# A decoder step on one core: page blocks side by side in the compression stage, low halves and bias copies on other engines, a third raw buffer

## What is computed

```
h = rmsnorm(x, norm_mix_g)                       # 1056 rows, transposed
cmp_rows = h @ w_in[:, cmp columns] + b_in       # 256 columns
# compression of every 32 rows (CMP_BLOCK) of keys and values, for the
# prompt's rows and for the 8 x 1024 past rows in paged caches
blk  = rows.reshape(B, nc, 32, 2, 2, 64) + pe[:, :, None, :]
flat = transpose(blk, (0, 1, 3, 4, 2, 5)).reshape(B, nc, 2, 2, 32 * 64)
hid  = gelu(einsum('bnzgf,zfe->bnzge', flat, w1))
out  = einsum('bnzge,zef->bnzgf', hid, w2)
```

## Time and profile before

| | |
|---|---|
| median of 3 runs | 2277.45 us (2276.51 to 2278.89) |
| the profiled execution, its own time | 2273.18 us |
| its span, first to last instruction | 2271.0 us |
| mean granted clock of TensorE | 0.957 |
| PE busy | 2137.8 us (94%) |
| DVE, ACT, POOL busy | 869.9, 686.7, 342.7 us |
| DMA | 153.41 MB, mean 68 GB/s |

### The profile page before, as it was taken

One profiled execution on the slowest core, in us unless ns is written; L12 is line 12 of the kernel. 1 busy time (PEld: TensorE's weight loads), 2 busy tenths in 40 slices (PEclk: granted clock), 3 DMA queues, 4 the chain that ended last, 5 costly groups with the idle time before them and its releaser, 6 DMA issues. The chain is left out here.

```text
span 2271.0 us, 36952 instructions
## 1 busy us (share of the span) xinstructions
PE 2137.8 (94%) x14615; PEld 1494.9 (66%) x14615; DVE 869.9 (38%) x1713; ACT 686.7 (30%) x1270; POOL 342.7 (15%) x253
## 2 busy tenths in 40 slices
PE   6999989799999998999999799886999999999998
PEld 5796645577777777556666566554666666666666
DVE  6321041465656564545334454233222222222223
ACT  4221232255555554362332233112111101101211
POOL 4300032400000000001011111004402501501400
PEclk8968999899999999999999899988999999999999
DMA  7601362211111102203102343311111111111101
GB/s 221 171 29 48 114 179 87 88 39 39 39 39 39 39 30 57 62 19 105 43 12 72 91 148 109 114 37 37 56 47 46 50 52 46 46 55 46 46 28 76
DMA packets 198941, 153.41 MB, mean 68 GB/s; under 512 B 10320, under 2 KB 185574, under 8 KB 198634
## 3 DMA queue, kind: packets, MB, share of 16 engines
q1 hardware_dynamic: 189386, 138.96, 20.6%
q0 software_dynamic: 4640, 10.60, 1.7%
q10 hardware_dynamic: 4800, 2.30, 0.3%
HBM read 124.66 MB, written 31.33 MB: 69 GB/s over the span
## 5 line engine op out<-in xcount | busy, mean ns | idle before, releaser
L318 PE MATMUL ps<-hH,wH 128*128 128x352 f16 x1584 | 324.8, 314 | 24.3 <-DVEq L283 19.9
L318 PE MATMUL ps<-hH,wL 128*128 128x352 f16 x1584 | 324.4, 314 | 0.0
L318 PE MATMUL ps<-hL,wH 128*128 128x352 f16 x1584 | 324.2, 314 | 0.0
L297 DVE SCALAR_TENSOR_TENSOR wL<-w,wH 128x1024 f16<-128x1024 f32 x98 | 120.0, 1225 | 288.6 <-ACT wH L290 273.1
L318 PEld LDWEIGHTS ps<-hH,wH 128*128 128x128 f16 x1584 | 154.9, 98 | 110.3 <-issue 25.3
L318 PEld LDWEIGHTS ps<-hL,wH 128*128 128x128 f16 x1584 | 155.3, 98 | 82.7
L318 PEld LDWEIGHTS ps<-hH,wL 128*128 128x128 f16 x1584 | 155.2, 98 | 82.4
L318 PE MATMUL ps<-mH,wH 128*128 128x352 f16 x960 | 196.4, 314 | 7.9 <-DVEq L283 6.9
L318 PE MATMUL ps<-mL,wH 128*128 128x352 f16 x960 | 196.1, 313 | 0.0
L318 PE MATMUL ps<-mH,wL 128*128 128x352 f16 x960 | 196.0, 313 | 0.0
L290 ACT ACTIVATE wH<-w 128x1024 f16<-128x1024 f32 x98 | 102.5, 1046 | 231.1 <-PE ps L318 225.4
(11 more groups left out here) (424 smaller groups left out, 3081.7 us busy)
## 6 DMA issues: line engine op xcount, KB each, us to landing
w<-in_mlp_w SPq DMA_DIRECT2D x64, 512.0 KB, 4.0
w<-in_w_in SPq DMA_DIRECT2D x36, 512.0 KB, 5.1
hH<-gates SPq DMA_DIRECT2D x24, 528.0 KB, 3.6
gates<-cmpT SPq DMA_DIRECT2D x20, 528.0 KB, 3.0
paw<-in_w_in SPq DMA_DIRECT2D x16, 512.0 KB, 4.6
hL<-in_w_branch SPq DMA_DIRECT2D x24, 256.0 KB, 3.7
xT<-xTd SPq DMA_DIRECT2D x1, 4224.0 KB, 12.9
fxn<-in_x_prompt SPq DMA_DIRECT2D x8, 512.0 KB, 5.8
```

The lines of the kernel that those rows point to most:

```text
L297: self.k.nc.vector.scalar_tensor_tensor(self.k.wL[:, slot % 2, :, :], self.k.w32[:, slot, :, :], WS, self.k.wH[:, slot % 2, :, :], ALU.mul ...
L318: ins = nc.tensor.matmul(k.ps[:, 3 * parity + c, 0:CH], w[:, kt, :], x[:, kt, c * CH:(c + 1) * CH], start=(kt == 0 and x is inH and w is w ...
```

## The change

In the second block the transposed pages are put elsewhere: PE writes the four transposes of a tile so that each PSUM bank of a pair of tiles holds one t with its columns in the order (z, block, row pair r); the copies read them as (z, r, block), that is at a step of 16 floats, and x2 becomes [P, 2, 2, PR, G * WBLK]. The stationary operand of a hidden sum is then x2[:, wave, z, r, :], 128 floats side by side. The prompt's xp is as it was.

In the first block: xr gets a third buffer (RO = 3); the low half hL is made by DVE, one iteration after tmp, and POOL only issues DMAs; brow is copied by ACT; seven of the 15 small vector loads move from POOL's queue to SP's, behind x_in(0); ACT squares tile t + 1 before the root of tile t, and the root stands before the raw copy; DVE makes the diagonal before its raw copy; the Newton step has two fewer one-column operations (one fused product, and the last factor is folded into the diagonal); four dense chunks instead of two stand in PE's tile loop, three of their evacuations in ACT's.

```diff
@@ front
-    NTILE, RING, XR = NB * PAGES // 2, 12, 5
+    NTILE, RING, XR, RO = NB * PAGES // 2, 12, 5, 3
...
-            xr, tmp = sb1("xr", [P, 2, KD, P]), sb1("tmp", [P, 3, KD, P])
+            xr, tmp = sb1("xr", [P, RO, KD, P]), sb1("tmp", [P, 3, KD, P])
@@ first block, SP
                 x_in(0)
+                for r, src, off, n in vectors[1::2]:
+                    sp.dma_start(vrows[r:r + n, :], bass.AP(tensor=src.tensor, offset=off, ap=[[P, n], [1, P]])).then_inc(more_loaded, 16)
@@ first block, POOL
-                for r, src, off, n in vectors:
+                for r, src, off, n in vectors[0::2]:
...
                 for t in range(NC):
-                    c = slice(t * P, t * P + rows[t])
-                    pool.wait_ge(hi_made, t + 1)
-                    nc.gpsimd.tensor_tensor(k.hL[:, :, c], tmp[:, t % 3, :, 0:rows[t]], k.hH[:, :, c], ALU.subtract).then_inc(lo_made, 1)
+                    pool.wait_ge(lo_made, t + 1)
@@ first block, PE
-                pe.wait_ge(loaded, 16 * 15)
+                pe.wait_ge(loaded, 16 * 8)
+                pe.wait_ge(more_loaded, 16 * 7)
...
-                    if t in (7, 8):
-                        dense(t - 7)
-                for e in range(2, 6):
+                    if t in (5, 6, 8, 9):
+                        dense(t - 5 if t < 7 else t - 6)
+                for e in range(4, 6):
                     dense(e)
@@ first block, ACT
+                square(0)
                 for t in range(NC + 2):
+                    if t + 1 < NC:
+                        square(t + 1)
                     if t < NC:
                         n = rows[t]
...
                         act.wait_ge(ms_made, t + 1)
                         nc.scalar.activation(root(t), ms(t), ACT.Sqrt).then_inc(root_made, 1)
+                        act.wait_ge(raw_turned, 2 * t + 1)
+                        if t >= RO:
+                            act.wait_ge(raw_out[t % RO], 16 * (t // RO))
+                        nc.scalar.copy(xr[:, t % RO, 0:4, 0:n], four(RAW, n)).then_inc(raw_act, 1)
...
                         nc.scalar.copy(k.hH[:, :, u * P:u * P + rows[u]], tmp[:, u % 3, :, 0:rows[u]]).then_inc(hi_made, 1)
+                        if u < H:
+                            act.wait_ge(bias_made, u + 1)
+                            nc.scalar.copy(brow[:, u, :], k.ps[:, BIAS + u % 2, 0:384]).then_inc(rows_made, 1)
+                    if t in (7, 8, 10):
+                        evacuate((0, 1, 2)[(7, 8, 10).index(t)])
@@ first block, DVE
                         settle(nc.vector.reciprocal(y(t), root(t)))
-                        settle(tt(t2(t), y(t), y(t), ALU.mult))
-                        settle(tt(t2(t), t2(t), ms(t), ALU.mult))
+                        settle(nc.vector.scalar_tensor_tensor(t2(t), y(t), y(t), ms(t), ALU.mult, ALU.mult))
                         settle(ts(t2(t), t2(t), -0.5, 1.5, ALU.mult, ALU.add))
-                        settle(tt(y(t), y(t), t2(t), ALU.mult))
...
-                        ts(diag[0:n, t % 2, 0:n], k.c('ident')[0:n, 0:n], y(t), None, ALU.mult).then_inc(diag_made, 1)
+                        ts(diag[0:n, t % 2, 0:n], k.c('ident')[0:n, 0:n], y(t), t2(t), ALU.mult, ALU.mult).then_inc(diag_made, 1)
...
+                    if t >= 2:
+                        u = t - 2
+                        c = slice(u * P, u * P + rows[u])
+                        dve.wait_ge(hi_made, u + 1)
+                        tt(k.hL[:, :, c], tmp[:, u % 3, :, 0:rows[u]], k.hH[:, :, c], ALU.subtract).then_inc(lo_made, 1)
@@ second block
-        x2 = sb("x2", [P, 2, 2, G, WBLK * PR])
+        x2 = sb("x2", [P, 2, 2, PR, G * WBLK])
...
-                    ins = nc.tensor.transpose(k.ps[:, n % 4, tz * P:(tz + 1) * P], pages[:, n % RING, tz * P:(tz + 1) * P], k.c('ident'))
+                    o = (2 * (tz % 2) + n % 2) * P
+                    ins = nc.tensor.transpose(k.ps[:, 2 * (m % 2) + tz // 2, o:o + P], pages[:, n % RING, tz * P:(tz + 1) * P], k.c('ident'))
...
-                    src = xp[:, z, r::PR] if u == PROMPT else x2[:, ORDER[u] % 2, z, :, r::PR]
+                    src = xp[:, z, r::PR] if u == PROMPT else x2[:, ORDER[u] % 2, z, r, :]
...
-                o = m % (TPW // 2) * 2 * P
+                o = g * WBLK + m % (TPW // 2) * 2 * P // PR
                 for t in range(2):
-                    src = k.ps[g * DH:(g + 1) * DH, 2 * (m % 2):2 * (m % 2) + 2, t * 2 * P:(t + 1) * 2 * P]
-                    copy(x2[t * DH:(t + 1) * DH, v % 2, :, g, o:o + 2 * P].rearrange("p z (b n) -> p z b n", b=2),
-                         src.rearrange("p b (z n) -> p z b n", z=2)).then_inc(tile_out[g], 1)
+                    src = k.ps[g * DH:(g + 1) * DH, 2 * (m % 2) + t, :]
+                    copy(x2[t * DH:(t + 1) * DH, v % 2, :, :, o:o + 2 * P // PR],
+                         src.rearrange("p (z b r) -> p z r b", z=2, r=PR)).then_inc(tile_out[g], 1)
```

More of the change, by code:

```diff
@@ L432, in front @@
     raw_turned, raw_act, raw_dve = k.sem("f_rturned"), k.sem("f_ract"), k.sem("f_rdve")
-    raw_out = [k.sem(f"f_rout{i}") for i in range(2)]
+    raw_out = [k.sem(f"f_rout{i}") for i in range(RO)]
     turned, scaled, hi_made, lo_made = k.sem("f_turned"), k.sem("f_scaled"), k.sem("f_hi"), k.sem("f_lo")
@@ L512, in _ @@
                 sp.wait_ge(rows_out, 16 * H)
-                sp.wait_ge(raw_out[0], 16 * 5)
-                sp.wait_ge(raw_out[1], 16 * 4)
+                for i in range(RO):
+                    sp.wait_ge(raw_out[i], 16 * (NC // RO))
             @block.gpsimd
             def _(pool):
[L518 to L523, removed]
-                for r, src, off, n in vectors:
+                for r, src, off, n in vectors[0::2]:
                     pool.dma_start(vrows[r:r + n, :], bass.AP(tensor=src.tensor, offset=off, ap=[[P, n], [1, P]])).then_inc(loaded, 16)
@@ L609, in evacuate, with square @@
                                          bias=k.vec[:, VB_CMP + i:VB_CMP + i + 1], scale=1 / WS).then_inc(evacuated, 1)
+                def square(t):
+                    n = rows[t]
+                    act.wait_ge(xl[t % XR], 16 * (t // XR + 1))
+                    if t:
+                        act.wait_ge(summed, t)
+                    nc.scalar.activation(xsq[0:n, :], xn[0:n, t % XR, :], ACT.Square, accum_out=k.sums[0:n, t:t + 1]).then_inc(summed, 1)
+                square(0)
                 for t in range(NC + 2):
+                    if t + 1 < NC:
+                        square(t + 1)
                     if t < NC:
                         n = rows[t]
-                        act.wait_ge(xl[t % XR], 16 * (t // XR + 1))
-                        if t:
-                            act.wait_ge(summed, t)
-                        nc.scalar.activation(xsq[0:n, :], xn[0:n, t % XR, :], ACT.Square, accum_out=k.sums[0:n, t:t + 1]).then_inc(summed, 1)
-                        act.wait_ge(raw_turned, 2 * t + 1)
-                        if t >= 2:
-                            act.wait_ge(raw_out[t % 2], 16 * (t // 2))
-                        nc.scalar.copy(xr[:, t % 2, 0:4, 0:n], four(RAW, n)).then_inc(raw_act, 1)
                         act.wait_ge(ms_made, t + 1)
                         nc.scalar.activation(root(t), ms(t), ACT.Sqrt).then_inc(root_made, 1)
-                    if t >= 2:
+                        act.wait_ge(raw_turned, 2 * t + 1)
+                        if t >= RO:
+                            act.wait_ge(raw_out[t % RO], 16 * (t // RO))
+                        nc.scalar.copy(xr[:, t % RO, 0:4, 0:n], four(RAW, n)).then_inc(raw_act, 1)
+                    if t < 2:
+                        act.wait_ge(w_in[t], 16)
+                        nc.scalar.activation(k.wH[:, t, :, :], k.w32[:, t, :, :], ACT.Copy, scale=WS).then_inc(w_hi, 1)
+                    else:
                         u = t - 2
```

49 lines of the change are left out of this document (26 added, 23 removed).

## The result

The changed kernel took 2239.74 us in the median (2235.33 to 2240.95), the kernel before 2277.18 (2276.51 to 2278.89) beside it: a ratio of 0.9831 [0.9814, 0.9848], 37.4 us less where 45 were forecast. The profiled execution took 2240.95 us, its span is 2239.3, and the mean granted clock 0.970 (0.957 before).

What follows compares the result with a forecast made beforehand. Bound by TensorE: strided weight loads and half clock in the second block, holes in the first. Gains 32.1 + 4.0 + 11 = 47.1, less 2.1, give 45 off the 2277.45 us median: 2232 us, range 2225 to 2256.

Steps and rivals of the forecast that it cites:

- Waves, 32.1 less: Second block's waves: contiguous weight loads at 0.11 us each with full clock, 47.0 us instead of 79.1.
- Tail, 4.0 less: Second block's tail, 10.6 us: some 8 of small matmuls and first projection tile halve at full clock, 4.0 less.
- First block, 11 less: First block: tiles 4.3 us apart, chunks filling PE's holes, end at 74.2 instead of 85.2; gain 11, bounds 6 and 13.
- I take 0 for the start, bounds -2 to +2: First block's start: delayed x and w loads against earlier page vectors from GpSimd's halved queue, net 0 us.
- The named threat: First block's start: seven small loads moved to SP delay issue of x 1 to 4 and both w tiles, about 3 us.
- Those queues are full anyway: First block's start: remark set against the about 3 us issue delay of x and w tiles; start taken as 0.
- GpSimd's page DMAs ... are issued by 65 and needed at 74: 0: First block's end: page loads, now behind VectorE's low halves, come in time for the second block and cost 0.
- slow copies: Rival, second block: copies out of PSUM slow to 1.32 us, wave 0 and clock lose 5 each, 2242 us; chance 0.07.
- copies as the bound: Rival, second block: VectorE copies set the pace, gain zero at 2.7 us each, 2285 us at 2.9; chance 0.02.
- it falls for a part: Rival, waves: clock falls to half for part of them, 2250 us if half the time; chance 0.17.
- A low start would not heal itself: Waves, argument against full clock: packed loads are no faster at half clock, so a low start would stay; no size.
- The 2.1 us allowance for other dense stages: Taken off the summed gain of 47.1 for one or two half-clock stretches, as dense stages have now and then.

Runs made afterwards that it cites:

- the rest before wave 1: Changed kernel with twelve VectorE fills of a scratch buffer that TensorE waits for ahead of wave 1 of the second block: 2249.58 us, ratio 0.9890.
- the later split: Changed kernel with ScalarE's two splits of w_in, and VectorE's low halves of them, two tiles later in its list: 2232.08 us, ratio 0.9824.
- both mended: Changed kernel with next stage's loads issued in the second block, GpSimd's weights issued behind the w_in splits, and the splits two tiles later: 2226.40 us, repeated 2224.19.
- the execution above: Profiled execution, 2248.94 us, of the changed kernel measured once more without edits (median 2241.99 us); clock at 0.50 for some 13 us of wave 3.

## Why the forecast was right, and what it got wrong

The sign, the place and the main size came out as argued: in the range, 7.7 us above the forecast. Step by step:

- **Waves, 32.1 less.** From the first page turn before the waves' sums (98.39 before, 94.47 after) to the last sum's end: 79.1 us became 135.29 + 7.33 - 94.47 = 48.15, where 47.0 were worked out, so 30.9 less. The pair of tiles takes 2.57 us (twice the 1.285 from one tile's first turn to the next's), forecast 2.64, which gives 0.8 back in 12 pairs. The hand-offs between the waves take some 2.9, such as the 1.17 us stand behind wave 2, where 1.2 in all were left. The prices of 0.11 a matmul and 0.20 at half clock are shown, the latter by the rest before wave 1. The gain has two parts, by an estimate from the kernel before's rows: 15 of its 24 page tiles in the waves ran at half clock, at 2.46 us instead of 2.13, so some 5 us of the 30.9 are the clock, and some 26 the shorter loads at full clock.
- **Tail, 4.0 less.** From the last sum to L318 it was 6.7 and is 4.7. L318 begins at half clock in both, for 4.1 us before and 2.4 now, worth 0.9. So 2.9. In most profiles here the clock falls in the tail, among its small dependent steps, and L318 begins at half clock in all but one; I had let all of it run at 1.00.
- **First block, 11 less: the step that failed.** It was 5.0 at the start of the second block, and 3.9 at its first wave sum (98.84 and 94.92), since the stand is followed by the lower clock (0.88 in the window from 81.05; with a stand of 0.90 us the same stretch takes 12.78 instead of 13.87). The forecast had the last dense matmul end at 74.2 us instead of 85.2; it ended at 77.0. By its parts: the tile loop was sized right or better (3.9 to 4.0 us a tile, forecast 4.3; from the end of tile 4's bias row, at 42.7, to the end of the last dense chunk, at 77.0, 34.3 us, forecast 37.2). What failed were two zeros.
  - *"I take 0 for the start, bounds -2 to +2".* Tile 4 was done at 42.7 instead of 37, as ScalarE stood 8.18 us for w_in, which it had 6.5 us later than before (20.82 and 14.34); the later split recovered 6.1. The named threat was there, but it was the smaller part of the cause: the seven small loads put w_in's issue off from 4.17 to 6.58 us, and moving them behind w_in brought it back by 1.3 us only. The larger part was the other side of the same move, which the forecast counted as a gain: GpSimd, with seven loads fewer ahead of it, issues the first of its 1 MB of weights at 6.83 us instead of 10.39, beside w_in; holding them back brought w_in 4.75 us earlier. "Those queues are full anyway" was taken as a cover where it was the cause.
  - *"GpSimd's page DMAs ... are issued by 65 and needed at 74: 0".* GpSimd waits for VectorE's low halves until 68.83 and then issues its last four pages one after another, the last at 72.97. Beside 2 MB of the next stage's weights that one takes 6.6 us to land. The block's end waits for it, 3.2 us more than before. In the kernel before the last page was issued as late, at 72.76, but TensorE was busy until 85.2, which hid it.

  With both mended TensorE's last dense matmul ends at 69.7 us and the second block starts at 70.6.
- **New waits and the third buffer.** VectorE's low half costs 1.21 us and never waits for ScalarE (idle 0.0 in its group), the bias copy on ScalarE fits. The third buffer, at 0 in the forecast, still leaves ScalarE's raw copies of tiles 4 and 5 standing 1.03 and 1.12 us for a store; with two buffers the gain of the block is gone.
- **The copies at a step of 16 floats: 0.** 694 ns before and after. The rivals that hung on it, slow copies and copies as the bound, are out. The Trainium skill, "PSUM — Partial Sum Buffer", Specifications, speaks of matmuls where it says that non-contiguous patterns slow them; the trace shows that it does not carry over to these engines' copies.
- **The clock.** "It holds through the waves" is right for eight of the ten profiles with the new layout (the made rest apart). The rival "it falls for a part" is real in the other two, for 6.5 us each and not the 18 that half of the waves would cost. It had the chance 0.17 as a whole outcome; it is rather something that befalls single executions, and part of why they spread from 2235 to 2249 us. Two of the forecast's arguments on it were wrong. "A low start would not heal itself": behind the made rest the clock was back some 3.6 us after the work began again, in the execution above after 13 us. And "no stretch of it is transposes alone": the kernel before has one at the start of its second block, 32 page turns with two short stands, through which the clock stays at 1.00 (the window counts a few matmuls of its neighbours at the edges):

```profile
86.25:91.30 5.05, 3.94 (x35) 3.52 (x33) 3.95 (x7) 3.47 (x6) 4.88 (x6) 1.00 0.19 52
```

  That the full clock comes with the new layout is shown by the two halves of the change, run alone (0.65 in the waves with the old places, 1.00 with the new); why it does is argued in the forecast and not shown.
- **Sum.** Front: 3.9 + 30.9 + 2.0 + 0.9 = 37.7 against 47.1. That the medians differ by 37.4 too is partly luck: the two profiled executions differ by 32.2 (2273.18 and 2240.95), the later stages of the second being 5.2 us longer. The 2.1 us allowance for other dense stages stays unproven. From L318 to the end thirteen profiles have between 2084.4 and 2092.8 us, the kernel before 2086.8, the changed kernel 2092.0 and 2092.3. That is on the side of "a cost of the change" in the expectation; but of nine profiles of variants with the new layout, whose later code is the same, eight lie at 2084.4 to 2089.7 and one, the two raw buffers, at 2092.8, and the medians differ by 33.9 to 37.4, so a cost of up to some 4 us in the later stages is neither shown nor ruled out. This stays open.

What each source is worth, by the runs: layout 31.8, first block 5.3, together 37.4; left on the table by start and end of the first block 13 to 18.

## What to carry to other kernels

When a stage is sped up, list what its last barrier waits for, transfers too: a load that was hidden behind the slow stage, however early its issue, may now be its end, and big prefetches beside it decide that. A wait for a large load belongs as late in an in-order list as its consumer allows; here moving the wait gained as much as moving the traffic. And a weight load that strides in SBUF can cost twice at full clock and nothing at half, so price it at both levels before giving it a value.

## What the runs showed of the hardware that I had not expected

- *Weight loads.* A matmul of 64 columns with 128 float weight columns at a step of 64 bytes takes 0.211 us at full clock, and with them side by side 0.105; at half clock both take 0.20. With 64 weight columns at that step, the prompt's, it is (112.07 - 104.84)/64 = 0.113 at full clock in the changed kernel, so the price goes with the number of strided columns. The Trainium skill, "SBUF — State Buffer", Door 1, says that SBUF reads in lines of 16 bytes and that each access that crosses to a new line pays a penalty; the trace agrees, with a factor of 2 for 128 columns. VectorE and ScalarE, reading PSUM and writing SBUF, paid nothing for the same step (694 and 579 ns).
- *The clock falls without a stand.* In the waves of the kernel before TensorE has no idle time from 91.30 us on, and at 102.65 its four transposes go from 0.61 to 1.01 us: half clock (the earlier trace rows show it later). So a full TensorE is no sign of a full clock.
- *The clock rises on transposes.* In the changed kernel the clock falls to 0.50 as the second block begins, behind 4.05 us of standing, and TensorE's next 24 instructions are page transposes (81.25 to 85.8). The windows:

```profile
84.00:85.00 1.00, 1.00 (x7) 0.73 (x6) 0.71 (x2) 0.48 (x2) 0.94 (x2) 0.63 0.43 131
85.00:86.00 1.00, 0.84 (x8) 0.60 (x6) 0.97 (x2) 0.97 (x2) 1.00 (x2) 1.00 0.26 70
```

It is at 1.00 from about 85 us on, before any other matmul. The rule of "TensorE: Matmul & The Clock Gate", Part 4, in the Trainium skill, that transposes don't count as PE-busy in the same way, is not borne out here for float transposes.
- *The same stand, two outcomes.* TensorE waits 1.16 or 1.17 us at wave 2's end in all ten profiles with the new layout. In nine the clock stayed at 1.00 behind it, in one 0.50 followed for 13 us. So the length of a single short stand does not tell what follows it, and whether it is the cause at all is not shown; only several executions tell what to expect.
- *What a block's end waits for.* The start of the next block came 1.44 us behind the landing of GpSimd's last DMA in all eight profiles in which TensorE stood long, and in the changed kernel it was ahead of the landing of SyncE's last prefetch load (81.05 and 82.2 us): that one is not waited for.
- *Order in one queue.* Seven loads with 35.5 KB behind 1 MB in SyncE's queue: the last was issued at 17.63 us instead of 4.15, and TensorE's instruction that needs them came at 22.28 instead of 10.87. Small transfers that something waits for go ahead of large ones.
